# A hybrid mLSTM, differential attention and mixture-of-experts block: the router rebuilt around the output projection, and the odd experts' up matrix held whole

## The chip, the cores and the metric

The kernel runs on one core of a Trainium2 chip. The metric is the time of one execution on the device in microseconds (us), as the median of several runs. A core has TensorE (PE, matmuls; PEld is its loading of the stationary operand), VectorE (DVE), ScalarE (ACT), GpSimd (POOL), SyncE (SP, which here issues nearly all the transfers) and 16 DMA engines.

## What is computed

The block takes 256 rows of 1024, with 16 meta tokens ahead of them, and runs two branches and a mixture of experts. The part that the change touches is the end of the first half and the experts:

```python
h = layer_norm(DN_ALPHA * h + merged @ w_out[l], ln1_g[l], ln1_b[l])
# group_moe
probs = softmax(xt @ w_router)
sel = probs + router_bias
group_score = max(sel.reshape(-1, 4, 4), axis=-1); top_group = argmax(group_score)
_, idx = top_k(where(in_group, sel, NEG), 2)
w = probs at idx, divided by their sum
for e in range(16):
    h = silu(xt @ w_gate[e]) * (xt @ w_up[e])
    y = y + combine[:, e:e + 1] * (h @ w_down[e])
h = layer_norm(DN_ALPHA * h + ffn, ln2_g[l], ln2_b[l])
```

All inputs are float32. Each expert's three matrices are 1024 x 1024, 4 MiB each.

## The kernel before

**Projections.** Nine 1024 x 1024 sections (XM, OG, KA, QA, VA, GA, GB, WM, WA) and the output projection run one after the other. A weight piece of 128 x 512 is split on ScalarE and VectorE into a high part `whi` and a low part `wlo` (lines 667 and 968; 727 and 1037 for the output projection), and TensorE forms three products for each (lines 1562 to 1564; 1791 to 1793). There are four buffers for pieces. Attention and the mLSTM scan lie between and inside the sections.

**Output projection and LN.** The sixteen pieces of `w_out` go by rows: piece n is row block n // 2, column half n % 2, so all four accumulators (two row tiles of 128 tokens, two column halves) end together. After the last piece VectorE adds the residual into `h1` (L1334), takes the statistics (L1323), GpSimd raises to -0.5 (L627), VectorE normalises (L1341), and TensorE transposes (L1804). The transposed `h1t` gets the LN gain and bias on its way out of PSUM, half on VectorE (L1346), half on ScalarE (L887).

**Router.** Logits come as 16 x 256 (L1812), are copied and transposed back to 128 tokens x 16 (L1826). `h1t` is transposed back too (L1819) so that `h1` holds the finished rows. VectorE softmaxes and picks group and two experts by a chain of small operations (`first_max`, lines 1360 to 1368, three times) up to `mask` (L1421). Five small products turn the mask into each token's rank in its expert (L1834 to L1838), from which come `slot`, and `pick`, the 0/1 matrix that gathers up to 64 tokens for a unit. `keep_warm` issues matmuls on `ident` whose results nobody reads (L1537).

**Experts.** A unit is one block of 64 tokens of one expert; here there are 16, one for each expert. For each TensorE does the gate product (32 matmuls, L1895), the gather for the next unit (L1855), the up product (32), the scatter of the unit before (L1847), transposes (L1862), and the down product (32). `s.gate_used`, `s.up_used` and `s.down_used` count quarters of a product; SyncE waits on them before it reloads a buffer. SyncE works through one list in order. Buffers: `raw` has one slot each for gate, up and down; `gate_x` is a second gate buffer for the odd experts; `up_x` is a second buffer for the left half of up (its first 512 rows) of the odd experts. The right half of up has one buffer, so it is fetched only when the expert before has used it. The order of the list for expert e is gate (e + 1 or e + 2), up left, up right, down. Ahead of the router SyncE issues gate 0, up 0, gate 1 and down 0, then the two parts of `up_x`; the second of these waits for `h1_back`, and everything else for `units_ready`.

## Time and profile before

| | |
|---|---|
| median of 3 runs | 842.73 us (841.73 to 843.7) |
| the profiled execution, its own time | 843.29 us |
| its span in the profile | 841.0 us |
| TensorE busy | 785.0 us, 93% of the span |
| VectorE, ScalarE, GpSimd busy | 344.8, 242.5, 23.6 us |
| bytes read from HBM | 249.91 MB, 298 GB/s over the span |
| granted TensorE clock, mean | 0.99 |
| the chain that ended last | PE 67%, DMA 24%, DVE 4% |

The span runs from the first to the last recorded instruction; the execution's own time is 2.3 us longer. The chain is followed back from the last instruction, at each step to what released it. Line numbers are those of the kernel before. Times of day in a row ("382.19") are microseconds from the start of the span.

### The profile page before, as it was taken

The page shows a single profiled execution, that of the slowest core. Times are in us where ns is not written, and L with a number is a line of the kernel's source. Part 1 is how long each engine was busy: PE and PEld are TensorE (multiplying, and loading weights), DVE is VectorE, ACT ScalarE, POOL GpSimd, SP SyncE. Part 2 cuts the span into 40 slices and gives each one's busy share as a digit, 9 for nine tenths or more (in the row PEclk, how much of TensorE's full clock was granted, in tenths as well). Part 3 has the DMA queues.
Part 4 walks back from the last instruction along what each step waited for, and adds up shares of the span by engine and source line. Part 5 has one row for each costly group of instructions (what it writes and reads, how often), then busy time and mean ns, then how long its engine had stood idle before and what let it go on. Part 6 is the DMA issues. An engine that isn't in the chain of part 4 may idle for free.

```text
span 841.0 us, 12805 instructions
## 1 busy us (share of the span) xinstructions
PE 785.0 (93%) x4566; PEld 472.4 (56%) x4567; DVE 344.8 (41%) x765; ACT 242.5 (29%) x527; POOL 23.6 (3%) x49
## 2 busy tenths in 40 slices
PE   4999999999999999998999999998999989989983
PEld 3998679998889999873333332332333323323331
DVE  6676446554666778463222211220222202202225
ACT  2454423445666655231111011101110111011100
POOL 2002000000001000000000000000000000000000
PEclk9999999999999999999999999999999999999997
DMA  8965040555013544955999999999999999999991
GB/s 249 386 231 200 4 197 1 199 199 200 2 43 159 200 180 149 394 227 212 372 429 427 429 428 428 429 428 427 429 426 427 430 425 429 428 427 429 425 396 50
DMA packets 36219, 251.28 MB, mean 299 GB/s; under 512 B 5377, under 2 KB 12626, under 8 KB 22882
## 3 DMA queue, kind: packets, MB, share of 16 engines
q1 hardware_dynamic: 34128, 249.71, 72.5%
q10 hardware_dynamic: 2066, 1.25, 0.5%
q8 instruction: 14, 0.23, 0.1%
q14 instruction: 11, 0.09, 0.0%
HBM read 249.91 MB, written 1.05 MB: 298 GB/s over the span
## 4 chain that ended last, share of the span: by engine, by line
PE 67%; DMA 24%; DVE 4%; ACT 2%; issue 2%; POOL 1%; DVEq 0%; POOLq 0%; SPq 0%; ACTq 0%
DMA raw<-in_w_up_e_dram 24%; PE ps L1895 24%; PE ps L1562 8%; PE ps L1563 7%; PE ps L1564 7%; PE ps L1847 2%; PE ps L1855 2%; PE ps L1537 1%; PE ps L1618 1%; PE ps L1614 1%; PE ps L1674 1%; PE ps L1862 1%; PE ps L1791 1%; PE ps L1793 1%; PE ps L1792 1%
## 5 line engine op out<-in xcount | busy, mean ns | idle before, releaser
L1895 PE MATMUL ps<-raw,xg 128*64 128x512 f32 x640 | 146.2, 605 | 17.9 <-DMA raw<-in_w_up_e_dram 12.5
L1562 PE MATMUL ps<-hi_h,whi 128*128 128x256 f32 (+1 forms) x448 | 129.6, 289 | 2.6 <-DVE wlo L968 2.5
L1564 PE MATMUL ps<-hi_h,wlo 128*128 128x256 f32 (+1 forms) x448 | 127.4, 284 | 0.0
L1563 PE MATMUL ps<-lo_h,whi 128*128 128x256 f32 (+1 forms) x448 | 127.2, 284 | 0.0
L1895 PE MATMUL ps<-raw,hid 128*64 128x512 f32 x512 | 113.4, 595 | 0.0
L968 DVE TENSOR_TENSOR wlo<-raw,whi 128x512 fp32r<-128x512 f32 x144 | 93.5, 691 | 47.1 <-ACT whi L667 44.4
L1895 PEld LDWEIGHTS ps<-raw,xg 128*64 128x64 f32 x640 | 45.6, 139 | 115.2 <-issue 85.7
L1562 PEld LDWEIGHTS ps<-hi_h,whi 128*128 128x128 f32 x448 | 84.4, 188 | 7.2 <-DVE wlo L968 3.7
L667 ACT CAST whi<-raw 128x512 fp32r<-128x512 f32 (+1 forms) x144 | 83.3, 619 | 13.6 <-PE ps L1564 11.9
L1489 DVE TENSOR_TENSOR gs<-ps,gsig 128x512 f32<-128x512 f32 x16 | 11.1, 692 | 183.8 <-ACT gsig L915 183.8
L1564 PEld LDWEIGHTS ps<-hi_h,wlo 128*128 128x128 f32 x448 | 84.5, 189 | 0.0
L1563 PEld LDWEIGHTS ps<-lo_h,whi 128*128 128x128 f32 x448 | 84.3, 188 | 0.0
L1895 PEld LDWEIGHTS ps<-raw,hid 128*64 128x64 f32 x512 | 35.3, 137 | 67.3 <-issue 62.2
L1492 DVE TENSOR_TENSOR hs<-ps,gs 128x512 f32<-128x512 f32 x16 | 11.1, 692 | 134.6 <-PE ps L1895 134.6
L1895 PE MATMUL ps<-gate_x,xg 128*64 128x512 f32 x256 | 57.1, 595 | 5.3 <-DMA gate_x<-in_w_gate_e_dram 5.2
L919 ACT COPY hid<-ps 128x512 f32<-128x512 f32 x16 | 9.4, 586 | 160.3 <-PE ps L1862 160.3
L921 ACT COPY zsb<-ps 128x512 f32<-128x512 f32 x16 | 9.4, 586 | 115.0 <-PE ps L1895 115.0
L1895 PEld LDWEIGHTS ps<-gate_x,xg 128*64 128x64 f32 x256 | 17.9, 137 | 43.7 <-issue 33.1
L1498 DVE TENSOR_TENSOR acc<-ps,acc 128x512 f32<-128x512 f32 x64 | 39.8, 684 | 5.6 <-PE ps L1847 5.6
L915 ACT ACTIVATE gsig<-ps 128x512 f32<-128x512 f32 x16 | 9.6, 597 | 93.9 <-PE ps L1895 93.9
L1847 PE MATMUL ps<-zsb,wpt 64*128 64x512 f32 x136 | 33.8, 615 | 0.8 <-ACT zsb L921 0.8
L1855 PE MATMUL ps<-h,pick 128*64 128x512 f32 x136 | 32.1, 593 | 0.0
(311 smaller groups left out, 975.0 us busy)
## 6 DMA issues: line engine op xcount, KB each, us to landing
raw<-in_w_down_e_dram SPq DMA_DIRECT2D x32, 2048.0 KB, 21.7
raw<-in_w_up_e_dram SPq DMA_DIRECT2D x24, 2048.0 KB, 24.7
raw<-in_w_gate_e_dram SPq DMA_DIRECT2D x16, 2048.0 KB, 23.4
gate_x<-in_w_gate_e_dram SPq DMA_DIRECT2D x16, 2048.0 KB, 23.2
raw<-in_w_in_dram SPq DMA_DIRECT2D x28, 1024.0 KB, 9.2
up_x<-in_w_up_e_dram SPq DMA_DIRECT2D x16, 1024.0 KB, 27.5
raw<-in_w_branch_m_dram SPq DMA_DIRECT2D x4, 1024.0 KB, 8.1
raw<-in_w_branch_a_dram SPq DMA_DIRECT2D x4, 1024.0 KB, 8.0
```

Of the source, the lines that this page charges most:

```text
L667: act.copy(whi[:, b, :].rearrange("p (k c) -> p k c", c=P), piece(section, blk, kh)).then_inc(s.hi_ready, 1)
L915: act.activation(gsig[:], ps[:, B_GATE, :], ACT.Sigmoid).then_inc(s.gsig_ready, 1)
L968: dve.tensor_tensor(wlo[:, b, :].rearrange("p (k c) -> p k c", c=P), piece(section, blk, kh), whi[:, b, :].bitcast(F32).rearrange("p (k c) ...
L1489: dve.tensor_tensor(gs[:], ps[:, B_GATE, :], gsig[:], ALU.mult).then_inc(s.gs_ready, 1)
L1492: dve.tensor_tensor(hs[:], ps[:, B_UP, :], gs[:], ALU.mult).then_inc(s.hs_ready, 1)
L1498: dve.tensor_tensor(acc[:, t, cols], ps[:, B_SCAT[j], :], acc[:, t, cols], ALU.add).then_inc(s.acc_added, 1)
L1562: mm(o, w1, hi[:, k, c0:c0 + n], start=(k == 0), stop=False)
L1563: mm(o, w1, lo[:, k, c0:c0 + n], start=False, stop=False)
L1564: last = mm(o, w2, hi[:, k, c0:c0 + n], start=False, stop=(k == KB - 1))
L1847: mm(ps[:, B_SCAT[j], :], wpt[r0:r0 + SLOTS, t, :], zsb[r0:r0 + SLOTS, :], start=True, stop=True).then_inc(s.scat_done, 1)
L1855: last = mm(ps[r0:r0 + SLOTS, B_GATH, :], pick[:, t, 0:SLOTS], h1[:, t, 512 * c:512 * c + 512], start=(t == 0), stop=(t == TT - 1))
L1895: last = mm(ps[r0:r0 + SLOTS, bank_no, :], lhs[:, k % 4, k // 4, :], w[:, k % 2, 512 * c:512 * c + 512], start=(k == 0), stop=(k == KB - 1))
```

## The change

- **Output projection by column halves.** Pieces 0 to 7 are the left 512 columns, 8 to 15 the right. `residual_half` and `stats_half` of the left half are placed among VectorE's last splits, the transposes of the left half ahead of the last piece.
- **Logits from the un-normalised sum.** `h1` is transposed before it is normalised. The LN gain is multiplied into `wr`, its column mean is taken out, and the LN bias becomes a row `rout_b`; this is done among the KA, QA and VA sections. Logits come as 128 tokens x 16 and are scaled by rstd on VectorE.
- **All pairs compared.** In place of the three `first_max` chains every pair of a group, and every pair of groups, is subtracted and compared once, and the wins are summed.
- **Norm scale at the gather.** ScalarE normalises `h1` in place; the gain and bias are applied to the gathered and transposed `xg` (now two operations for each unit), and, spread over 128 partitions by 16 matmuls (`rows_b`), to `acc` in eight operations ahead of the loop. `h1` is no longer transposed back.
- **Up matrix whole.** `up_x_left` and two `up_x_right` buffers hold the whole up matrix of the odd experts. It is issued ahead of the router, and in the loop the order is gate, up, down. The two LN rows for the end move from ScalarE's list into SyncE's, behind the last expert.

The diff, cut to its core:

```diff
+    ht = at("ht", [P, KB, T], F + 8192)
...
-    up_x = (at("up_x0", [P, 2, D], split_area + 8192 - work),
-            at("up_x1", [P, 2, D], 0))
+    up_x_left = at("up_x_left", [P, 4, D], 0)
+    up_x_right = (at("up_x_right0", [P, 2, D], split_area + 8192 - work),
+                  at("up_x_right1", [P, 2, D], F + 23072))
...
-        for q, (read, n) in enumerate(((s.pieces_used, OUT_BASE + PIECES + NBUF), (s.h1_back, 2 * TT))):
-            sp.wait_ge(read, n)
-            sp.dma_start(flat(up_x[q][:]), flat(four_rows(w_up[0, 1], 0)[:, 2 * q:2 * q + 2, :])).then_inc(up_x_in[q], 16)
+        sp.dma_start(flat(up_x_right[1][:]), flat(four_rows(w_up[0, 1], 1)[:, 2:4, :])).then_inc(up_x_in[2], 16)
+        sp.wait_ge(s.pieces_used, OUT_BASE + PIECES + NBUF)
+        sp.dma_start(flat(up_x_left[:]), flat(four_rows(w_up[0, 1], 0))).then_inc(up_x_in[0], 16)
+        sp.dma_start(flat(up_x_right[0][:]), flat(four_rows(w_up[0, 1], 1)[:, 0:2, :])).then_inc(up_x_in[1], 16)
...
+        def fetch_up(e, odd):
+
+            last = last_block(e - 2)
+            sp.wait_ge(s.up_used, last * 4 + 2)
+            if odd:
+                sp.dma_start(flat(up_x_left[:]), flat(expert_rows(w_up, e, 0))).then_inc(up_x_in[0], 16)
+                for j in range(2):
+                    sp.wait_ge(s.up_used, last * 4 + (j + 3))
+                    sp.dma_start(flat(up_x_right[j][:]), flat(expert_rows(w_up, e, 1)[:, 2 * j:2 * j + 2, :])
+                                 ).then_inc(up_x_in[1 + j], 16)
+            else:
+                sp.dma_start(flat(raw_half(ESLOT[1], 0)), flat(expert_rows(w_up, e, 0))).then_inc(raw_in[ESLOT[1]][0], 16)
+                sp.wait_ge(s.up_used, last * 4 + 4)
+                sp.dma_start(flat(raw_half(ESLOT[1], 1)), flat(expert_rows(w_up, e, 1))).then_inc(raw_in[ESLOT[1]][1], 16)
+
+        def fetch_down(e):
+
             last = last_block(e - 1)
...
+        with sp.Fori(0, NE // 4 - 1) as i:
+            for odd in range(2):
+                fetch_gate(i * 2 + (2 + odd), odd)
+                fetch_up(i * 2 + (2 + odd), odd)
+                fetch_down(i * 2 + (1 + odd))
...
+        sp.wait_ge(s.gate_used, last_block(NE - 1) * 4 + 4)
+        for j, v in enumerate((ln2_g, ln2_b)):
+            sp.dma_start(rows1[:, j, :], v[0].partition_broadcast(P)).then_inc(s.rows2_in, 16)
...
-        for k in range(4, KB):
...
-        act.wait_ge(s.logit_done, 1)
-        act.copy(lgt[:], ps[0:NE, 4, 0:T]).then_inc(s.logit_sb, 1)
+        for b in range(4):
+            if b == 2:
+
+                act.activation(table_load[:], neglam[0:1, :], ACT.Exp)
+            act.wait_ge(s.ht_t1, b + 1)
+            act.copy(ht[:, 2 * b:2 * b + 2, :], turned1[:, 2 * b:2 * b + 2, :]).then_inc(s.ht_ready, 1)
+
...
-            for half in range(2):
-                act.wait_ge(s.h1_back, 2 * t + half + 1)
-                act.copy(h1[:, t, 512 * half:512 * half + 512], ps[:, 2 * t + half, :]).then_inc(s.h1_ready, 1)
-        for t in range(TT):
-            act.wait_ge(s.h1_ready, 2 * t + 2)
-            act.mul(acc[:, t, :], h1[:, t, :], ALPHA).then_inc(s.acc_ready, 1)
-
-        for j, v in enumerate((ln2_g, ln2_b)):
-            act.dma_start(rows1[:, j, :], v[0].partition_broadcast(P)).then_inc(s.rows2_in, 16)
+            act.activation(h1[:, t, :], h1[:, t, :], ACT.Identity, bias=nmr[:, t:t + 1],
+                           scale=rstd[:, t:t + 1]).then_inc(s.h1_ready, 1)
...
+        dve.wait_ge(s.wr_in, 16)
+        own(dve.tensor_tensor(wr_b[:], wr[:], l1b, ALU.mult))
+        own.settle()
+        own(dve.tensor_tensor(wr[:], wr[:], l1g, ALU.mult))
+        own(dve.tensor_reduce(rout_sum[:, 1, :], wr_b[:].rearrange("p k e -> p e k"), AX.X, ALU.add))
+        own.settle()
+        dve.tensor_reduce(rout_sum[:, 0, :], wr[:].rearrange("p k e -> p e k"), AX.X, ALU.add).then_inc(s.rout_in, 1)
...
+        dve.wait_ge(s.rout_done, 1)
+        dve.scalar_tensor_tensor(out=wr[:], in0=ps[:, 7, 0:NE].unsqueeze(1).to_broadcast([P, KB, NE]), scalar=-1.0 / D,
+                                 in1=wr[:], op0=ALU.mult, op1=ALU.add).then_inc(s.wr_ready, 1)
+        dve.tensor_copy(rout_b[:], ps[:, 7, NE:2 * NE]).then_inc(s.wr_ready, 1)
...
+        def residual_half(t, c):
+            dve.scalar_tensor_tensor(out=h1[:, t, 512 * c:512 * c + 512], in0=hres[:, t, 512 * c:512 * c + 512],
+                                     scalar=ALPHA, in1=ps[:, 4 + 2 * t + c, :], op0=ALU.mult,
+                                     op1=ALU.add).then_inc(s.resid_done, 1)
+
...
         for n in range(2, PIECES):
             split_out(n)
+            if n == KB + NBUF - 1:
+                dve.wait_ge(s.pieces_used, OUT_BASE + KB + NBUF)
+                residual_half(0, 0)
+            elif n == KB + NBUF:
+                residual_half(1, 0)
+            elif n in (KB + NBUF + 1, KB + NBUF + 2):
+                stats_half(n - (KB + NBUF + 1), 0)
+        dve.wait_ge(s.pieces_used, OUT_BASE + PIECES + NBUF)
+        for t in range(TT):
+            residual_half(t, 1)
+        for t in range(TT):
+            stats_half(t, 1)
+        own.settle()
+        for t in range(TT):
+            own(dve.bn_aggr(mv[:, t, :], stats[:, t, :, :]))
+        own.settle()
+        dve.tensor_scalar(ve[:, 0:TT], mv[:, 0:TT, 1], EPS, None, ALU.add).then_inc(s.var1, 1)
...
-        for t in range(TT):
...
-            dve.wait_ge(s.rstd1, t + 1)
-            dve.tensor_scalar(h1[:, t, :], h1[:, t, :], mv[:, t, 0:1], rstd[:, t:t + 1],
-                              ALU.subtract, ALU.mult).then_inc(s.xn1_ready, 1)
...
+        def take_gathered(n):
+            dve.tensor_tensor(xg[:], ps[:, B_XT, :].rearrange("p (a c s) -> p a c s", c=2, s=SLOTS), by_slot(gain4),
+                              ALU.mult).then_inc(s.xg_scaled, 1)
+            dve.wait_ge(s.xg_scaled, n)
+            dve.tensor_tensor(xg[:], xg[:], by_slot(bias4), ALU.add).then_inc(s.xg_ready, 1)
...
+        for t in range(TT):
+            own(dve.scalar_tensor_tensor(out=rt[:, 0, NE * t:NE * t + NE], in0=ps[:, t, 0:NE], scalar=rstd[:, t:t + 1],
+                                         in1=rout_b[:], op0=ALU.mult, op1=ALU.add))
         own.settle()
         dve.tensor_reduce(rt[:, 15, 0:TT], val(0), AX.X, ALU.max, negate=True).then_inc(s.router_exp, 1)
+        dve.wait_ge(s.rb_in, 16)
...
+        own(dve.tensor_reduce(best, sel8, AX.X, ALU.max))
+        own(dve.tensor_tensor(pair8, sel8.unsqueeze(2).to_broadcast([P, TG, EPG, EPG]),
+                              sel8.unsqueeze(3).to_broadcast([P, TG, EPG, EPG]), ALU.subtract))
+        own.settle()
...
+        dve.tensor_scalar(mask_b[:], val(12), 2.0, None, ALU.is_lt).then_inc(s.mask_ready, 1)
...
+        dve.wait_ge(s.rows_b, 1)
+        for t in range(TT):
+            for c in range(2):
+                cols = slice(512 * c, 512 * c + 512)
+                own(dve.scalar_tensor_tensor(out=acc[:, t, cols], in0=ps[:, 6 + c, :], scalar=ALPHA,
+                                             in1=h1[:, t, cols], op0=ALU.mult, op1=ALU.mult))
...
+        pe.wait_ge(s.rout_in, 1)
+        mm(ps[:, 7, 0:2 * NE], one[:].to_broadcast([P, P]), rout_sum[:].rearrange("p a e -> p (a e)"), start=True,
+           stop=True).then_inc(s.rout_done, 1)
...
+        def logits(half):
+
+            for k in range(4 * half, 4 * half + 4):
+                pe.wait_ge(s.ht_ready, max(k // 2 + 1, 2))
+                for t in range(TT):
+                    last = mm(ps[:, t, 0:NE], ht[:, k, P * t:P * t + P], wr[:, k, :], start=(k == 0), stop=(k == KB - 1))
+            return last
+
         for n in range(PIECES):
-            k, half = divmod(n, 2)
-            pe.wait_ge(s.mg_lo_s, k + 1)
+            half, k = divmod(n, KB)
...
+            if n == PIECES - 2:
+
+                pe.wait_ge(evac[WM], KB + 2)
+                pe.wait_ge(evac[WA], KB + 2)
+                turn_half(0)
+        logits(0)
+        turn_half(1)
+        logits(1).then_inc(s.logit_done, 1)
+
+
+        for r, b in ((C_L1G, (6, 7)), (C_L1B, (2, 4))):
+            for k in range(KB):
+                last = mm(ps[:, b[k // 4], P * (k % 4):P * (k % 4) + P], ident[0:81, r + k:r + k + 1].to_broadcast([81, P]),
+                          crow[:], start=True, stop=True)
+        last.then_inc(s.rows_b, 1)
+
+        keep_warm(5, 10)
 
         pe.wait_ge(s.mask_ready, 1)
         g = dict(skip_group_check=True)
-        mm(ps[:, 6, 0:NE], before[:], mask[:, 0, :], start=True, stop=True, **g)
...
+        ones_b = one_b[:].to_broadcast([P, P])
+        mm(ps[:, 5, 0:2 * NE], before_b[:], mask_b[:].rearrange("p t e -> p (t e)"), start=True, stop=False, **g)
+        mm(ps[:, 5, NE:2 * NE], ones_b, mask_b[:, 0, :], start=False, stop=True, **g)
+        mm(ps[:, 5, 2 * NE:3 * NE], ones_b, mask_b[:, 0, :], start=True, stop=False, **g)
+        mm(ps[:, 5, 2 * NE:3 * NE], ones_b, mask_b[:, 1, :], start=False, stop=True, **g).then_inc(s.rank_done, 1)
...
```

The VectorE program between the KA and the QA section (names: `stats`, `mv`, `ve` are the statistics of the mLSTM heads, `hh` their output). Before:

```order
L1190 BN_STATS stats_75<-hh 128x6
L1201 BN_AGGR mv_76<-stats_75 128x2 x8
L1203 TENSOR_SCALAR ve_77<-mv_76 128x8
L1011 UNCONDITIONAL_BRANCH
L1011 ISA
L968 ISA
L968 TENSOR_TENSOR wlo<-raw,whi 128x512
```

and now:

```order
L1205 BN_STATS stats_82<-hh 128x6
L1218 TENSOR_TENSOR wr_b<-wr,chan 128x128
L1220 TENSOR_TENSOR wr<-wr,chan 128x128
L1221 TENSOR_REDUCE rout_sum<-wr_b 128x16
L1223 TENSOR_REDUCE rout_sum<-wr 128x16
L1225 BN_AGGR mv_83<-stats_82 128x2 x8
L1227 TENSOR_SCALAR ve_84<-mv_83 128x8
```

Four operations have come in ahead of the aggregation, and so ahead of QA's next split.

The TensorE program from the last pieces of the output projection to the first gather (`h_135` and `h_142` are `h1`). Before:

```order
L1791 MATMUL ps<-whi,mg_hi 128x512
L1792 MATMUL ps<-whi,mg_lo 128x512
L1793 MATMUL ps<-wlo,mg_hi 128x512
L1537 MATMUL ps<-ident 128x128 x26
L1804 MATMUL ps<-ident,h_135 128x128 x16
L1812 MATMUL ps<-h1t,wr 16x256 x8
L1819 MATMUL ps<-ident,h1t 128x128 x8
L1826 MATMUL ps<-ident,lgt 128x16 x2
L1819 MATMUL ps<-ident,h1t 128x128 x8
L1537 MATMUL ps<-ident 128x128 x26
L1834 MATMUL ps<-mask,before 128x16
```

and now:

```order
L1870 MATMUL ps<-wlo,mg_hi 128x512
L1848 MATMUL ps<-ident,h_142 128x128 x8
L1868 MATMUL ps<-whi,mg_hi 128x512
...
L1870 MATMUL ps<-wlo,mg_hi 128x512
L1857 MATMUL ps<-wr,ht 128x16 x8
L1848 MATMUL ps<-ident,h_142 128x128 x8
L1857 MATMUL ps<-wr,ht 128x16 x8
L1884 MATMUL ps<-crow,ident 128x128 x16
L1592 MATMUL ps<-ident 128x128 x10
L1893 MATMUL ps<-mask_b,before_b 128x32
```

Half of the transposes now stand ahead of the last piece, those back are gone, and 16 products with `crow` and 10 on `ident` stand ahead of the rank products.

SyncE's list in the first lap of the loop, from gate to down. Before:

```order
L507 DMA gate_x<-in_w_gate_e_dram 128x4096
...
L526 DMA raw<-in_w_up_e_dram 128x4096
...
L530 DMA raw<-in_w_up_e_dram 128x4096
L532 REGISTER_ALU
L533 DMA raw<-in_w_down_e_dram 128x4096 x2
```

and now:

```order
L521 DMA gate_x<-in_w_gate_e_dram 128x4096
...
L532 DMA up_x_left<-in_w_up_e_dram 128x4096
L534 REGISTER_ALU
L535 DMA up_x_right_168<-in_w_up_e_dram 128x2048
...
L535 DMA up_x_right_169<-in_w_up_e_dram 128x2048
```

The odd expert's up matrix has moved into buffers of its own, so its right half no longer waits for the expert before; down follows it.

## Rows read from the trace of the kernel before

**Rows 1.** Windows: us; busy us of PE, PEld, DVE, ACT, POOL; PEclk, DMA share, GB/s.

```profile
378.00:386.00 8.00, 5.78 (x28) 2.09 (x26) 4.78 (x19) 1.87 (x2) 0.00 (x0) 1.00 0.00 2
382.20:408.00 25.80, 25.80 (x122) 9.49 (x124) 8.60 (x21) 1.77 (x3) 0.00 (x0) 1.00 0.72 268
386.00:389.00 3.00, 3.00 (x16) 1.04 (x14) 0.60 (x2) 0.00 (x0) 0.00 (x0) 1.00 0.72 208
408.00:816.00 408.00, 386.04 (x1788) 134.55 (x1786) 82.61 (x171) 54.00 (x74) 0.00 (x0) 0.99 1.01 428
818.00:819.00 1.00, 1.00 (x7) 0.39 (x8) 1.00 (x3) 0.00 (x0) 0.00 (x0) 1.00 0.27 115
```

**Rows 2.** Timeline, SyncE's queue: start, length, issue; x2 are two transfers.

```profile
349.62 0.80 SPq L487 DMA_DIRECT2D raw<-in_w_down_e_dram  x2
353.84 15.60 SPq L492 DMA_DIRECT2D up_x<-in_w_up_e_dram  x2
385.88 3.77 SPq L510 DMA_DIRECT2D raw<-in_w_gate_e_dram  x2
...
785.35 0.33 SPq L530 DMA_DIRECT2D raw<-in_w_up_e_dram  x1
```

**Rows 3.** The chain that ended last: start us, us, what.

```profile
442.61 6.87 PE ps L1895 x32
...
468.42 6.87 PE ps L1895 x32
...
811.12 3.65 PE ps L1895 x16
...
818.07 7.08 PE ps L1895 x32
```

**Rows 4.** Timeline of the router and first unit: start, us, engine, line, operation.

```profile
353.85 1.28 DVE L1334 SCALAR_TENSOR_TENSOR h<-hres,ps 128x512 f32<-128x512 f32 x2 [4.25 <-PE ps L1793]
...
362.04 1.09 PE L1804 MATMUL ps<-ident,h 128*128 128x128 f32 x8 [0.59 <-DVE h L1341]
...
368.33 0.19 DVE L1394 TENSOR_REDUCE rt<-rt 128x2 f32<-128x32 f32 x1
...
368.92 5.97 PE L1537 MATMUL ps<-ident 128*128 128x128 f32 x52
...
369.27 0.17 DVE L1397 RECIPROCAL rt<-rt 128x2 f32<-128x2 f32 x1 [0.76 <-ACT rt L895]
...
374.05 0.19 DVE L1421 TENSOR_TENSOR mask<-rt 128x32 f32<-128x32 f32 x1
...
374.73 0.29 PE L1834 MATMUL ps<-mask,before 128*128 128x16 f32 x2
...
375.95 0.19 DVE L1431 SCALAR_TENSOR_TENSOR slot<-ps,mask 128x32 f32<-128x32 f32 x1 [0.97 <-PE ps L1838]
...
377.28 1.94 PE L1855 MATMUL ps<-h,pick 128*64 128x512 f32 x8
...
380.69 0.69 DVE L1388 COPY xg<-ps 128x512 f32<-128x512 f32 x1 [1.46 <-PE ps L1862]
...
382.19 7.09 PE L1895 MATMUL ps<-raw,xg 128*64 128x512 f32 x32 [1.53 <-DVE xg L1388]
...
391.03 0.59 ACT L917 COPY xsb<-ps 128x512 f32<-128x512 f32 x1 [1.12 <-PE ps L1855]
```

**Rows 5.** Timeline: a small VectorE operation, and the start of QA.

```profile
22.97 0.29 DVE L1069 TENSOR_TENSOR lamp<-lamv 128x128 f32<-128x128 f32 x1
...
156.50 1.30 DVE L968 TENSOR_TENSOR wlo<-raw,whi 128x512 fp32r<-128x512 f32 x2 [2.11 <-POOL rstd L622]
...
157.25 0.39 PE L1562 MATMUL ps<-hi_h,whi 128*128 128x256 f32 x1 [0.49 <-DVE wlo L968]
```

**Rows 6.** Timeline of TensorE after a wait, and a window in it.

```profile
526.74 5.35 PE L1895 MATMUL ps<-raw,xg 128*64 128x512 f32 x16 [2.96 <-DMA raw<-in_w_up_e_dram]
...
528.00:529.00 1.00, 1.00 (x6) 0.31 (x4) 0.00 (x0) 0.00 (x0) 0.00 (x0) 0.50 1.08 459
```

287 lines of the change are left out of this document (126 added, 161 removed).

## The prediction

> **What bounds the kernel now.** I read the page's slices first, for where DMA is full, and then cut windows there. The program has two parts: up to 353.85 us TensorE streams projections, and from 408 us on the expert stage runs with saturated DMA, 428 GB/s over 408 to 816 us; the stream falls off in the window 818 to 819 [rows 1]. An expert has three matrices of 4 MiB. TensorE needs 25.81 us for a unit (442.61 to 468.42, from one up product to the next, where it waited for nothing) [rows 3], but 12 MiB at 428 GB/s take 29.4 us. The bytes are the bound, TensorE is not, and the end is
>
> (start of the first unit) + (bytes still to be moved) / rate + (time in which DMA moved nothing or little) + tail.
>
> I call the start of the first gate product s; before, s = 382.19 [rows 4]. The queue rows show what was loaded ahead of it: gate 0, gate 1, up 0, down 0 and the left half of up 1 in two parts (353.84 lasts to 369.4 because the second part waits for `h1_back`) [rows 2], 18 MiB. 174 MiB are left, 182.5 MB, 426.3 us at 428 GB/s. Lost after s: 3.8 us until 386 (the first gate buffer comes free at 385.88 [rows 2]), then 25.80 us ran at a mean of 268 GB/s from 382.2 to 408, which is 9.6 us of lost rate in all, the 3.8 included [rows 1]. The sum, 382.2 + 426.3 + 9.6 = 818.1, agrees with the fall-off in 818 to 819 [rows 1], so I trust this account. The tail: the last wait is for the right half of up 15, which was issued last but two (785.35 [rows 2]) and whose products start at 811.12; the last down product takes 818.07 to 825.15 [rows 3], and 15.85 us of output work follow to 841.0. By the byte account up 15's right half ends 4 MiB (9.8 us) before 818.3, at 808.5; TensorE went on 2.6 us later. I keep this 2.6 as the lag between a transfer's place in the byte account and its use.
>
> **The change, part by part.**
>
> *Router weights during the streams.* VectorE gets four operations on 128 x 128 elements between the last statistics of KA and the aggregation that QA waits for. One of that size is busy for 0.29, with the step to the next some 0.3 [rows 5]: 4 x 0.3 = 1.2 us. There VectorE is on the path: its wlo starts at 156.50 and TensorE waits for it until 157.25 [rows 5]. So +1.2. The small product with `rout_sum` adds one matmul between QA and VA, 0.23 (as a warm-up matmul, 5.97 / 26 [rows 4]). VectorE then waits for it, but has the length of a VA block as cover, so 0; without cover it would be 0.5. Together +1.45, and TensorE is busy from there to 353.85, so it all arrives. The added constants and small DMAs at the very start lie beside the wait for x and its statistics, with which TensorE starts: 0.
>
> *Output projection by halves.* The same 96 matmuls; the first half's residual and statistics move into VectorE's idle time, 0.64 each (1.28 for two [rows 4]) between the splits; the half is finished eight pieces ahead of the end, and a piece is six products of 512 columns, so there is room: 0, and 0.64 if the last split were late by one. Eight transposes go ahead of the last piece: 1.09 [rows 4] on TensorE, in the path.
>
> *Router.* Without the 1.45, from 353.85 [rows 4]: +1.09 = 354.94. Two residual halves (1.28) to 356.2; meanwhile the first 8 logit products, 0.23 each as the warm-up row, to 356.8. Eight transposes, 1.09, to 357.9; two copies of 128 x 512 on ScalarE, 0.59 each [rows 4], to 359.1; the last four logit products to 360.0. Variance and rstd run beside this on VectorE and GpSimd and are done by about 359. After the logits there are two races. VectorE: two scale-and-add and one maximum (0.65), exponentials and return 0.94 (as before between maximum 368.33 and reciprocal 369.27 [rows 4]), then up to the mask 8 small operations at 0.217 (369.27 to 374.05 were 22 of them [rows 4]) and three of 128 elements at 0.3, 2.7 us: mask at 364.3, where it took 4.8 before. TensorE: 16 matmuls that spread the gains plus 10 warm-up ones, 26 in all as before, 5.97 [rows 4]: until 366.0. TensorE is later, so 1.7 of what VectorE saves is lost; if a matmul with a broadcast stationary row costs half, the mask decides at 364.3. I take 366.0, since the form is nearest to the warm-up row. Four rank products instead of five: 1.22 (374.73 to the slot operation at 375.95) becomes 0.8 (bounds 0.6, half for the narrower type, and 1.0, four fifths): 366.8. Slot to gather was 1.33 (375.95 to 377.28) and loses one small operation: 367.9. Gather to first product was 4.91 (377.28 to 382.19 [rows 4]). The second operation of `take_gathered`, 0.69, lies in the 0.8 between xg's end at 381.38 and 382.19, in which TensorE was still reading its registers: 0, at most 0.7. So 372.8, and with the 1.45, **s = 374.3, 7.9 us earlier.**
>
> *Up matrix whole.* Before s there are now 20 MiB: at 351 us down 0 and one quarter of up 1, from 356.4 the other three. 8 MiB take 19.6 us and are through at about 373, ahead of s + 3.7. In place of 174, 172 MiB remain after s: 180.4 MB, 421.4 us. In each lap the order is gate, up, down. By the rows of the first unit the buffers come free at s + 3.7, 7.4 (gate), 12.3, 15.7 (up), 22.6, 26.4 (down), and 2 MiB take 4.9 us; starting at s + 5.35 the transfers end at 10.3, 15.2, 20.1, 25.0, 29.9, 34.8, each after the next is issued. So what the stretch to 408 lost besides vanishes (between 389 and 408, while up 1's right half and down 1 were issued into an empty queue), and only the first loss stays: 3.8 plus 3 us at 208 GB/s, 1.55 [rows 1]: 5.35. Last byte: 374.3 + 5.35 + 421.4 = 801.05.
>
> *Tail.* Up 15 now comes ahead of down 15, but down 15 is issued only when down 14 is used. TensorE's last wait is thus for down 14, which has 8 MiB behind it: 801.05 - 19.6 + 2.6 = 784.05. Then half a down product (3.5), a whole unit (25.8) and 15.85 of output: 829.2. Up 15 (793.9) and down 15 (803.7) arrive before they are wanted (796 and 806). The tail after the last byte grows from 22.9 to 28.15 us, and takes back part of the gain. The two LN rows (1 MiB) move behind down 15, 2.5 us, needed 20 us later: 0. The eight operations that form `acc` (8 x 0.69) end at s + 11, the scatter needs them at s + 15.7: 0.
>
> *Sum.* -7.9 (s) -4.9 (2 MiB) -4.25 (lost rate: 9.6 - 5.35) +5.25 (tail) = -11.8; 829.2 against 841.0. The profiled execution took 843.29 with a span of 841.0, the median of the runs is 842.73, 1.73 over the span. I predict 842.7 - 11.8, **831.0 us**.
>
> Beside this stands a page. "DMA: Bandwidth & Descriptors" of the Trainium skill (Anatomy of one DMA) gives each transfer a fixed cost of about 2.0 us, mostly between the last byte and the semaphore. Put in for my 2.6, which this trace shows, it would make 830.4, by that page's figure.
>
> **Rivals.**
>
> 1. *The queue still runs dry in the first laps.* For it: my transfers end only about a microsecond after the next issue in the first unit (down 1 at s + 26.4 against 29.9, gate 3 at s + 29.7 against 34.8, and up 1's half at 23.8 to 25.0 against 22.6). Against: with each lap 3.6 us of backlog are added. One of the two dips (4.25 / 2 = 2.1 us) or both: 833 to 835.5.
>
> 2. *The half clock.* After a wait of 3 us TensorE ran sixteen products in 5.35 us instead of 3.65 (526.74 against 811.12) [rows 3, 6], with a granted clock of 0.50 at 528 to 529 [rows 6], the 1.2 GHz level. Now each unit waits 3.6 us for down, and after down 14 there is no slack: +1.7. Of 58 matmuls that only kept TensorE busy around the router 48 are gone; if the first gate product ran at half clock, its first buffer would come free up to 3.5 us later. 832.5 to 836. "TensorE: Matmul & The Clock Gate" (What's actually happening) of the Trainium skill says that the throttled state is the default and activity lifts it; the row at 526.74 agrees. Against it: the wait splits in two (2.2 for the first half of down, 1.4 for the second), and the longest gap that I find in the new router is 1 us.
>
> 3. *Slower.* SyncE serves its list strictly in order, and down now stands behind the whole up matrix of the next expert. If a unit's down is issued with nothing in the queue, every expert pays a restart of about 2.1 us: 14 x 2.1 = 29 us against the 11.8, 848. It decides from the sixth restart on. Against it: at that point the queue holds gate and up of the next expert, 8 MiB or 19.6 us by my schedule.
>
> 4. *No change.* The stage is bound by bytes, so a faster router would be worth nothing if DMA's restart did not hang on it. But 378 to 386 shows 2 GB/s [rows 1], and 385.88 is the first gate buffer's release: the restart does hang on s.
>
> **How the numbers follow.** The forecast 0.77, rival 1 0.10, rival 2 0.07, rival 3 0.04, rival 4 0.02. The forecast's own spread: 1.7 less if the mask decides the rank, 2.6 less if the lag at down 14 is nothing, 0.7, 0.64 and 0.5 more for the covers that I priced at nothing: 827 to 833. With rivals 1 and 2: 825.5 to 836. A difference of 0.2% (1.7 us) is about what this kernel's runs can tell. Faster by more 0.94, within 0.02, slower 0.04.
>
> **What would show it.** First gate product at 374 to 375; TensorE late by 1.4 at the start of the output projection; DMA idle only until s + 3.8, with no window under 400 GB/s from s + 7 on; last byte near 801; down 14's second half as the last DMA in the chain, and 45 us from there to the end. Wrong if s is late because the added VectorE work costs more than 1.45, if DMA windows in the first laps dip, or if the last units wait for anything but down.

## The result, and the profile after

The median went from 842.73 to **838.21 us** (five runs, 835.42 to 838.64), a ratio of 0.9934 with an interval of 0.9913 to 0.9955. The forecast was 831.0 us with a range to 836.0: the direction was right, the gain is 4.5 us where 11.7 were forecast, and the time lies outside the range. The profiled execution took 835.89 us with a span of 834.1.

The expert stage first, since the account of [rows 1] rests on it. These are windows of the kernel after; the columns are as there:

```profile
374.00:382.90 8.90, 6.49 (x30) 2.43 (x32) 6.61 (x27) 1.87 (x2) 0.00 (x0) 1.00 0.01 4
383.00:386.00 3.00, 3.00 (x16) 1.04 (x14) 2.20 (x5) 0.00 (x0) 0.00 (x0) 1.00 0.70 191
...
389.00:408.00 19.00, 18.95 (x92) 7.16 (x90) 7.19 (x14) 2.46 (x3) 0.00 (x0) 1.00 1.00 428
408.00:806.00 398.00, 378.72 (x1762) 135.95 (x1760) 91.50 (x183) 52.13 (x72) 0.00 (x0) 0.99 1.01 428
806.00:809.00 3.00, 3.00 (x16) 1.06 (x14) 0.77 (x2) 0.00 (x0) 0.00 (x0) 1.00 0.83 336
```

DMA is idle until SyncE gets the first gate buffer at 382.94, needs three microseconds to come up, and then moves 428 GB/s from 389 to 806 with no dip in the first laps. The last weight bytes land near 806, the norm's two rows behind them. In this stage TensorE waits for one matrix only, down; the second line is its wait ahead of the first gate product. The waits are given by cause (us in total, times, longest), then the chain that ended last:

```profile
PE ps L1952 <- DMA raw<-in_w_down_e_dram: 18.9, 12, 2.1
...
PE ps L1952 <- DVE xg L1413: 1.7, 1, 1.7
```

```profile
757.92 25.63 DMA raw<-in_w_down_e_dram
783.55 0.04 issue
783.59 15.65 PE ps L1952 x64
...
811.18 7.11 PE ps L1952 x32
```

The chain enters TensorE's last unbroken stretch by down 14's transfer at 783.59, and not by an up half as before [rows 3]. That matrix was forecast, but this is its first half, 50.5 us from the end; the forecast had the second half, and 45 us. The timeline there and a window in it, and below them the same two products in experiment 9:

```profile
783.59 8.78 PE L1952 MATMUL ps<-raw,hid 128*64 128x512 f32 x32 [2.08 <-DMA raw<-in_w_down_e_dram]
```

```profile
784.00:788.00 4.00, 4.00 (x14) 1.20 (x12) 0.60 (x2) 0.00 (x0) 0.00 (x0) 0.57 1.01 430
```

```profile
775.87 3.65 PE L1961 MATMUL ps<-raw,hid 128*64 128x512 f32 x16 [1.84 <-DMA raw<-in_w_down_e_dram]
780.76 3.65 PE L1961 MATMUL ps<-raw,hid 128*64 128x512 f32 x16 [1.23 <-DMA raw<-in_w_down_e_dram]
```

In the kernel after the granted clock is down behind this wait, as rival 2 had it, and the two halves take 8.78 us without a wait between them. In experiment 9 the clock stays up and TensorE waits 1.23 us for the second half instead. From the start of the first half to the end of the span it is 50.5 us and 50.3: the half clock there takes 0.2 us and not 1.7, since it runs in time that would be a wait.

Now the router: the timeline of the kernel after, to be held against [rows 4]. A float32 matmul leaves two records here, so x32 is 16 of them and x20 is 10; a transpose or a bf16 matmul leaves one.

```profile
357.00 1.85 PE L1857 MATMUL ps<-wr,ht 128*128 128x16 f32 x16
358.70 1.07 PE L1848 MATMUL ps<-ident,h 128*128 128x128 f32 x8
360.22 2.94 PE L1857 MATMUL ps<-wr,ht 128*128 128x16 f32 x16 [0.46 <-ACT ht L912]
363.00 7.17 PE L1884 MATMUL ps<-crow,ident 81*128 81x128 f32 x32
369.96 3.00 PE L1592 MATMUL ps<-ident 128*128 128x128 f32 x20
372.80 0.18 PE L1893 MATMUL ps<-mask_b,before_b 128*128 128x32 bf16 x1
...
374.04 1.94 PE L1913 MATMUL ps<-h,pick 128*64 128x512 f32 x8 [0.99 <-DVE pick L1397]
...
379.09 5.37 PE L1952 MATMUL ps<-raw,xg 128*64 128x512 f32 x24 [1.68 <-DVE xg L1413]
```

```profile
366.96 0.18 DVE L1463 TENSOR_SCALAR mask_b<-rt 128x32 bf16<-128x32 f32 x1
...
373.09 0.19 DVE L1470 SCALAR_TENSOR_TENSOR slot<-ps,mask 128x32 f32<-128x32 f32 x1 [5.54 <-PE ps L1896]
```

```profile
360.00:362.00 2.00, 1.78 (x12) 1.78 (x12) 0.33 (x2) 0.66 (x2) 1.42 (x3) 0.75 0.94 401
362.00:370.00 8.00, 8.00 (x39) 8.00 (x39) 3.21 (x18) 2.95 (x6) 0.00 (x0) 0.50 1.02 431
370.00:372.00 2.00, 2.00 (x14) 2.00 (x14) 0.00 (x0) 0.00 (x0) 0.00 (x0) 0.69 0.94 397
```

The windows are read for their third column from the end, the granted clock: 0.75 over two microseconds is one microsecond at half clock, so the clock fell at about 361.0, stayed at 0.50 (the 1.2 GHz level) and came back at about 371.2 (0.69 over the last two). TensorE was busy in nearly all of that time. The 16 row matmuls took 7.17 us and the 10 warm-up ones 3.00, from 363.0 to 372.8 together 9.8, where I had put 5.97. VectorE had the mask at 367.14 and then waited 5.54 us. The first gate product, s in the prediction, starts at 379.09 and not at 374.3.

### The profile page after: what moved, and what is told of

Same layout as the page of the kernel before. It is cut to its first block, busy times and chain, and to the rows that moved or that the text cites. A ratio compares the mean times of both kernels' runs of the same rounds, so it can differ in the third digit from the quotient of the medians.

```text
span 834.1 us, 12681 instructions
## 1 busy us (share of the span) xinstructions
PE 779.0 (93%) x4496; PEld 474.1 (57%) x4497; DVE 357.6 (43%) x780; ACT 240.8 (29%) x523; POOL 22.7 (3%) x51
## 4 chain that ended last, share of the span: by engine, by line
PE 71%; DMA 21%; DVE 3%; ACT 2%; issue 2%; POOL 1%; DVEq 0%; POOLq 0%; SPq 0%; ACTq 0%
PE ps L1952 26%; DMA raw<-in_w_down_e_dram 21%; PE ps L1617 8%; PE ps L1619 7%; PE ps L1618 7%; PE ps L1905 2%; PE ps L1913 2%; PE ps L1673 1%; PE ps L1920 1%; PE ps L1669 1%; PE ps L1729 1%; PE ps L1592 1%; PE ps L1868 1%; PE ps L1870 1%; PE ps L1869 1%
## 5 line engine op out<-in xcount | busy, mean ns | idle before, releaser
L1952 PE MATMUL ps<-raw,hid 128*64 128x512 f32 x512 | 119.6, 618 | 19.4 <-DMA raw<-in_w_down_e_dram 18.9
L1952 PE MATMUL ps<-raw,xg 128*64 128x512 f32 x512 | 112.7, 592 | 1.7 <-DVE xg L1413 1.7
L1952 PEld LDWEIGHTS ps<-raw,xg 128*64 128x64 f32 x512 | 37.3, 137 | 73.8 <-issue 73.8
```

The costliest lines, as they stand in the source:

```text
L1952: last = mm(ps[r0:r0 + SLOTS, bank_no, :], lhs[:, k % 4, k // 4, :], w[:, k % 2, 512 * c:512 * c + 512], start=(k == 0), stop=(k == KB - 1))
```

## The experiments

The times of one kernel scatter here by several microseconds between its own runs, and the profiled start of the kernel by 1.9. So beside each median stand three figures of the profile: s, the start of the first gate product; the span; and their difference, which the scatter ahead of s does not touch. "Half clock in the router" is worked out from windows of 1 us, as above. Each kernel's median stands with its lowest and highest run; the kernel before, run beside them, had medians of 843.0 to 843.4. The expectations were reckoned from 838.21 for the kernel after; all nine of its runs (the five above and the four of experiment 11) have the median 835.89, 2.3 us less.

| kernel | median, runs | ratio to before (interval) | half clock in the router | s | span | span - s |
|---|---|---|---|---|---|---|
| before | 842.73 | | none | 382.19 | 841.0 | 458.8 |
| after | 838.21 (835.42 to 838.64) | 0.9934 (0.9913 to 0.9955) | 10.2 | 379.09 | 834.1 | 455.0 |
| 1 warm-up first | 832.84 (831.26 to 835.87) | 0.9874 (0.9857 to 0.9891) | 3.4 | 374.51 | 831.3 | 456.8 * |
| 2 no warm-up | 835.80 (832.66 to 837.00) | 0.9896 (0.9880 to 0.9912) | 13.7 | 377.74 | 834.3 | 456.6 * |
| 3 warm-up in the middle | 833.21 (831.41 to 839.22) | 0.9885 (0.9860 to 0.9911) | none | 374.50 | 831.3 | 456.8 * |
| 4 fetch order of before | 837.65 (835.83 to 842.30) | 0.9939 (0.9918 to 0.9959) | 10.2 | 379.38 | 837.6 | 458.2 |
| 5 gaps filled with rows | 830.53 (827.80 to 831.56) | 0.9842 (0.9826 to 0.9858) | 6.8 | 374.29 | 829.1 | 454.8 |
| 6 plain operand | 838.59 (832.96 to 838.73) | 0.9944 (0.9929 to 0.9959) | 6.8 | 376.20 | 831.4 | 455.2 |
| 7 gaps filled, warm-up | 832.16 (830.86 to 833.94) | 0.9874 (0.9857 to 0.9890) | 3.4 | 374.26 | 829.2 | 454.9 |
| 8 VectorE work moved | 835.39 (833.44 to 836.28) | 0.9909 (0.9894 to 0.9924) | 10.2 | 376.72 | 831.7 | 455.0 |
| 9 best | 827.92 (827.51 to 828.47) | 0.9823 (0.9809 to 0.9836) | none | 371.43 | 826.2 | 454.8 |
| 10 full rows | 832.60 (831.29 to 835.84) | 0.9884 (0.9865 to 0.9902) | none | 373.33 | 830.0 | 456.7 * |
| 11 after again | 835.69 (833.48 to 838.58) | 0.9905 (0.9890 to 0.9920) | 13.7 | 379.98 | 836.8 | 456.8 * |
| 12 before, less warm-up | 847.55 (846.03 to 848.16) | 1.0057 (1.0043 to 1.0070) | 6.8 | 383.44 | 843.8 | 460.4 * |

The star marks profiles in which the clock was down in the first gate product as well.

My theory: the changed router lets TensorE's clock fall, and its 16 row matmuls do not bring it back. Rivals: a fall has its own length whatever is issued; the fetch order gave less than forecast; the start of the kernel became slower.

**1. The warm-up first.**

```diff
+        keep_warm(5, 10)
         for r, b in ((C_L1G, (6, 7)), (C_L1B, (2, 4))):
...
-        keep_warm(5, 10)
```

> The kernel after with one move: the 10 warm-up matmuls stand ahead of the 16 matmuls that repeat the norm's rows, not behind them; the same 26 matmuls in all. In the kernel after these 26 took 9.8 us (363.0 to 372.8) with the granted clock at 0.50 until about 370.7, and the rank product behind them was 5.7 us later than VectorE's mask. Theory A (the clock comes back when the warm-up's plain 128x128 matmuls run, and the 16 broadcast matmuls do not bring it back): back at full clock about 0.7 us into the warm-up, near 364; the 26 take about 6.5 us, rank product near 369.5, time 3.0 to 3.4 us under the kernel after: 835.0. Theory B (once fallen, the clock stays down for some 10 us whatever is issued): full clock again near 370.7 as before, rank product at 372.8, time 838.2.

Timeline of TensorE, and a window with its granted clock:

```profile
360.71 3.80 PE L1592 MATMUL ps<-ident 128*128 128x128 f32 x20
364.30 4.09 PE L1886 MATMUL ps<-crow,ident 81*128 81x128 f32 x32
368.22 0.18 PE L1893 MATMUL ps<-mask_b,before_b 128*128 128x32 bf16 x1
...
374.51 8.78 PE L1952 MATMUL ps<-raw,xg 128*64 128x512 f32 x32 [1.68 <-DVE xg L1413]
```

```profile
375.00:379.00 4.00, 4.00 (x14) 1.30 (x12) 2.33 (x7) 0.00 (x0) 0.00 (x0) 0.57 0.01 4
```

The same 26 matmuls take 7.5 us, and the 16 row matmuls run at full speed once the clock is back. A fall has no fixed length, so theory B falls. Four of the five runs lie under the fastest of the nine runs of the kernel after (833.48), the fifth does not. New is a second fall, in the first gate product: 8.78 us instead of 7.09 [rows 4], and span - s is 1.8 larger.

**2. No warm-up:** the line `keep_warm(5, 10)` is taken out.

> The kernel after without its 10 warm-up matmuls in the router (no result comes from them). The 16 row matmuls end at 370.2 at half clock; VectorE's mask is there at 367.1, so the rank product starts at 370.2 instead of 372.8. Theory A (it was the warm-up that brought the clock back): half clock goes on through the rank product, the gather and the turn into the first gate product, which gives back 0.7 to 1.5 us: 836.3 to 837. Theory B (the clock comes back at about 370.7 by itself): the 2.6 us are gained whole: 835.6.

```profile
361.00:374.00 13.00, 12.01 (x53) 9.60 (x53) 6.27 (x38) 2.95 (x6) 0.45 (x2) 0.50 0.94 398
```

The clock does not come back by itself at 371; it stays down through the rank product and the gather, and falls again in the first gate product. By the windows this is theory A. The time alone does not tell: 835.80 is nearer to B's 835.6 than to A's 836.3 to 837, and it equals the 835.89 of the nine runs of the kernel after, so the 2.6 us that the matmuls took are not gained. Nor is the length of the fall by itself the mark of the missing warm-up, since experiment 11 has 13.7 us with the warm-up in place.

**3. Warm-up in the middle.**

```diff
         logits(0)
+        keep_warm(3, 8)
         turn_half(1)
```

> The kernel after with 8 more warm-up matmuls (0.23 us each at full clock, 1.84 us) between the first and the second half of the logits, where the clock was still full. Theory A (the stretch of transposes and 16-column products lets the clock fall): with the 8 in its middle the clock stays at 1.00 through the router, the 26 matmuls take 5.97 instead of 9.8 us, so 1.84 paid and 3.8 gained: 836.2, and the granted clock 1.00 from 357 to 380. Rival (the fall has another cause, as the DMA's 430 GB/s beside it): the clock falls anyway and the time is 840.0.

```profile
357.00:375.00 18.00, 14.19 (x115) 11.92 (x116) 10.11 (x49) 5.90 (x10) 1.42 (x3) 1.00 0.84 355
```

At full clock the 26 matmuls took 362.32 to 368.21, 5.9 us: the 5.97 of my prediction, with DMA as busy as in the kernel after, so it isn't DMA that holds the clock down. One of the six runs took 839.22. It has no profile, but its mean granted clock, 0.978 over a span of 837.5 against 0.987 over 831.3, makes some 15 us more of half clock (2 x 0.022 x 837.5 = 37 against 22). Where these lay is not recorded; if in the router, the eight matmuls don't always suffice. And experiment 10 below shows no fall in the router without them, so one profile does not prove that they hold the clock.

**4. The fetch order of before**, with the changed router: an odd expert's second up half waits for the previous expert's up product again, and expert 1's is not prefetched.

```diff
-                fetch_gate(i * 2 + (2 + odd), odd)
-                fetch_up(i * 2 + (2 + odd), odd)
-                fetch_down(i * 2 + (1 + odd))
...
+            fetch_gate(i * 2 + 3, True)
+            fetch_rest(i * 2 + 2, False)
+            fetch_gate(i * 2 + 4, False)
+            fetch_rest(i * 2 + 3, True)
```

> The kernel after with the fetch order of the kernel before: an odd expert's up matrix arrives in its own buffers still, but the second half is issued only behind the previous expert's up product, in two transfers, expert 1's second half is not prefetched, and the gate is asked for ahead of it as in the kernel before. The router is the changed one. My sum gives the whole up matrix 4.9 (2 MiB already there) + 4.25 (no loss at the laps' start) - 5.25 (longer tail) = 3.9 us, so 842.1. Rival (the fetch order is worth nothing, all of the gain is the router's): 838.2. Rival (the order costs as much as the router gave): above 844.

TensorE's waits in the expert stage, in us, times, longest:

```profile
PE ps L1956 <- DMA up_x_right<-in_w_up_e_dram: 8.6, 5, 3.0
PE ps L1956 <- DMA raw<-in_w_up_e_dram: 5.0, 4, 1.8
PE ps L1956 <- DMA gate_x<-in_w_gate_e_dram: 4.7, 5, 1.2
```

The waits for up and gate are back and that for down is gone. Span - s is 458.2 against 455.0: the new order is worth **3.2 us**, where my terms made 4.9 + 4.25 - 5.25 = 3.9. The medians do not show it as well: 837.65 is far from my 842.1, nearer to the first rival's 838.2, and 1.8 above the 835.89 of the nine runs, with runs from 835.83 to 842.30. By span - s neither rival holds; by the time alone the first would not be excluded.

**5 and 7. TensorE's gaps filled.** 7 puts plain warm-up matmuls into the three gaps behind the rank product; 5 puts the row matmuls there, and only 12 matmuls stay ahead of the rank product.

```diff
         keep_warm(5, 10)
+        norm_rows(0, 2)
...
+        norm_rows(2, 6)
...
         pe.wait_ge(s.pick_ready, TT)
...
         gather()
+        norm_rows(6, 9)
...
         turn_rows(B_XT, xsb[:], s.xt_done)
+        norm_rows(9, 2 * KB)
```

(7: `keep_warm(1, 4)`, `(1, 3)` and `(1, 7)` in these places, all 16 rows behind the first warm-up.)

> The kernel after with its 10 warm-up matmuls ahead, and the 16 row matmuls (whose result is needed only when the accumulator is built) spread: 2 behind the warm-up, 4 behind the rank product, 3 behind the gather, 7 behind the turn of the gathered rows, so in TensorE's gaps of 0.99, 0.69 and 1.68 us. In the run with the warm-up first the rank product was ready to start 4.0 us after the logits' end (VectorE's mask, near 364.8) but TensorE came to it at 368.2, and the clock fell again for 3.3 us at 375.6 in the first gate product (about 1.7 us lost). Theory A (work with gaps and narrow products lets the clock fall, each fall costs what is done in it at half speed): rank product near 365.5, no fall near 375, first gate product 3 us earlier than 374.5 and at full clock, time 4 to 5 us under 832.8: 828. Rival (the fillers delay the chain as much as they give, and the fall comes anyway): 831 to 833.

> The kernel with the warm-up first (832.8) plus plain warm-up matmuls in TensorE's gaps of the router's end: 4 behind the rank product (0.92 us in a gap of 0.99), 3 behind the gather (0.69 in 0.69), 7 behind the turn (1.6 in 1.68). Nothing on the path should be later by more than 0.2 us. Theory A: the fall of 3.3 us at 375.6 in the first gate product, which cost about 1.7 us, goes: 831.2, granted clock 1.00 from 365 to 390. Rival (that fall has nothing to do with the gaps): 832.8, the fall stays.

Windows of 7, then of 5:

```profile
365.00:388.00 23.00, 22.88 (x137) 12.17 (x137) 13.95 (x42) 3.05 (x4) 0.00 (x0) 1.00 0.70 282
```

```profile
361.00:367.00 6.00, 6.00 (x29) 6.00 (x30) 2.84 (x17) 2.96 (x6) 0.57 (x2) 0.50 1.01 429
368.00:388.00 20.00, 19.81 (x109) 9.14 (x109) 13.95 (x42) 3.05 (x4) 0.00 (x0) 1.00 0.72 291
```

With the gaps filled there is no second fall in either, and the first gate product takes 7.09 again; beside experiment 1 span - s is 1.9 us less. That the filling did it is not shown: of the ten profiles with these gaps as they were, six have the second fall and four (after, 4, 6, 8) have not, and the three with filled gaps (5, 7, 9) have none. By medians 7 gains 0.7 on experiment 1, half of what I expected, and 5, with 830.53, missed the 828 of theory A and lies just under its rival's 831. In 5 the first fall lasted 6.8 us in this profile although the warm-up began at 362.9, so the rank product came at 367.93 and not at 365.5; one of its runs had 827.80.

**6 and 10. What the 16 matmuls are.** 6 uses a plain piece of the identity, `ident[0:81, :]`, in place of the repeated column; 10 makes each of the 16 a product of the 128 x 128 identity with itself. Both leave out the norm's rows, so what follows works on other values.

> The kernel after with a plain 81x128 piece of the identity as the stationary operand of the 16 row matmuls, in place of one column of it repeated 128 times: same count, same moving operand, same shape of the product, other values (the rows of the norm's gain and bias, and with them the accumulator, are then wrong; all timing stays). Theory A1 (it is the repeated column that doesn't bring the clock back): full clock again some 3.5 us after the fall at 361, near 364.5, the 16 and the 10 behind them end near 369.8, rank product 3 us earlier than 372.8, time 835.2 against 838.2. Theory A2 (it is not the operand; the clock comes back only at the warm-up's 128-row matmuls or 10 us after the fall): half clock until 370.7 as before, time 838.2.

> The kernel after with each of its 16 row matmuls replaced by a plain product of the 128x128 identity with itself into the same place (the norm's rows, and with them the accumulator, are left out), so 26 full 128-row matmuls stand behind the logits. Theory A2 (matmuls of 81 rows do not bring the clock back, those of 128 do): half clock from 361 ends near 364.5 to 367, the 26 end at 368 to 370 instead of 372.8, time 833 to 835.5, and no run at 838. Rival (the kind of matmul does not matter, only when the fall begins): times of both kinds as before, 835.5 and 838.4, and the row matmuls' stretch at half clock for 7 us again.

```profile
360.76 6.16 PE L1884 MATMUL ps<-crow,ident 81*128 81x128 f32 x32
366.72 3.35 PE L1592 MATMUL ps<-ident 128*128 128x128 f32 x20
```

```profile
357.00:373.00 16.00, 12.52 (x101) 10.53 (x100) 9.96 (x48) 6.13 (x12) 1.42 (x3) 1.00 0.98 415
373.00:377.00 4.00, 3.67 (x10) 1.18 (x12) 3.15 (x10) 0.05 (x1) 0.00 (x0) 0.57 0.06 20
```

In 6 (rows above first) the clock came back at 368.7, 2.0 us into the warm-up and not at 364.5: with the plain piece, too, the clock stayed down as long as the row matmuls ran, so the repeated column is not the reason, and A1 falls. Its six runs are two of 833.0 and four of 838.6. In 10 no run lies above 835.84, and in its profile the clock did not fall until 373.0, just ahead of the first gate product, though its program is that of the kernel after until 361.15. That agrees with A2, that matmuls of 81 rows do less for the clock; but A2 expected a fall at 361 that ends early, and there was none. Since whether a fall comes differs from run to run, and the values differ too, experiments 6 and 10 do not prove that it is the 81 rows.

**8. The VectorE work moved.** The router's four operations between KA and QA stand behind the signal for the heads' rstd, in VectorE's wait for GpSimd.

```diff
-        own(dve.tensor_tensor(wr_b[:], wr[:], l1b, ALU.mult))
...
         dve.tensor_scalar(ve8[:], mv8[:, :, 1], EPS, None, ALU.add).then_inc(s.var8, 1)
+        own(dve.tensor_tensor(wr_b[:], wr[:], l1b, ALU.mult))
...
         dve.wait_ge(s.rstd8_ready, 1)
```

> The kernel after with the router's four VectorE operations between the KA and the QA section moved behind the signal for GpSimd's rstd of the heads, into the wait for it (2.1 us). My term of +1.2 us for this insertion: the QA section's evacuations come 1.2 us earlier by the trace (162.4 to 161.2 against the KA ones), so does all behind them, time 1.2 under the kernel after: 837.0 (in the trace the piece 7 signal 356.0 where the start of the kernel is the same). Rival (the insertion hides behind TensorE, and the 1.2 us is lost elsewhere): 838.2 and no shift.

VectorE in the kernel after, and then in this one:

```profile
154.19 0.29 DVE L1218 TENSOR_TENSOR wr_b<-wr,chan 128x128 f32<-128x128 f32 x1
...
158.38 1.29 DVE L983 TENSOR_TENSOR wlo<-raw,whi 128x512 fp32r<-128x512 f32 x2 [2.11 <-POOL rstd L642]
```

```profile
153.06 0.65 DVE L1216 BATCH_NORM_AGGREGATE mv<-stats 128x2 f32<-128x6 f32 x8
...
156.02 1.29 DVE L983 TENSOR_TENSOR wlo<-raw,whi 128x512 fp32r<-128x512 f32 x2 [0.88 <-POOL rstd L642]
```

From the first operation behind KA's statistics (there the first of the four, at 154.19, here the aggregation, at 153.06) to the next wlo it is 4.19 us there and 2.96 here, 1.23 less; VectorE's wait shrinks by as much, from 2.11 to 0.88. From the first product to the output projection's end it is 333.0 and 331.8. That is my term of 1.2, and it is on the path. The medians, 835.39 against 835.89, are too scattered to show it.

**9. Best:** experiment 5, with 8's edit, and `keep_warm(6, 4)` between `turn_half(1)` and `logits(1)`.

> The version that puts together what the runs showed: warm-up ahead and the 16 row matmuls in TensorE's gaps (830.5), the four VectorE operations behind the signal for the heads' rstd (1.25 us earlier by the trace), and 4 more warm-up matmuls (0.92 us) between the second turn and the second half of the logits, of which 0.46 lies in a wait. Theory A: if these 4 keep the clock up through the logits, the second half of them takes 1.96 instead of 2.96 us and the warm-up ends before the mask: first gate product at 371.5 to 372, time 827.5. Rival (the clock falls anyway, only later): the VectorE move alone counts, less the 0.46: 829.7.

```profile
360.88 2.48 PE L1592 MATMUL ps<-ident 128*128 128x128 f32 x20
...
365.07 0.19 PE L1899 MATMUL ps<-mask_b,before_b 128*128 128x32 bf16 x1 [1.27 <-DVE mask_b L1463]
```

```profile
357.00:388.00 31.00, 29.56 (x182) 16.79 (x183) 19.76 (x68) 7.09 (x12) 1.42 (x3) 1.00 0.87 362
```

827.92 us where 827.5 was expected, 1.8% under the kernel before, and the five runs lie within 1.0 us where those of the kernel after span 3.2, and all nine of them 5.2. The rank product now waits for VectorE's mask, so TensorE is no longer late. The clock is full from 357 to 388. Which of the two additions did how much was not separated: if 1.2 of the 2.6 under experiment 5 is 8's, the rest is the 4 matmuls' or the runs' own difference.

**11. After again.**

> The kernel after, unchanged, to see what differs between its own executions. If the start of the kernel is noise (x's landing and the moment when the clock first rises), the first evacuation will stand anywhere within 1.8 us of the 27.5 seen, without a change of code; end minus first gate product should be 455.0 where that product runs at full clock and 456.8 at half. Time: 835.5 or 838.4, median 837.

```profile
362.73 7.17 PE L1884 MATMUL ps<-crow,ident 81*128 81x128 f32 x32
369.70 4.16 PE L1592 MATMUL ps<-ident 128*128 128x128 f32 x20
...
379.98 8.36 PE L1952 MATMUL ps<-raw,xg 128*64 128x512 f32 x30 [1.68 <-DVE xg L1413]
```

This profile is of an 838.58 run: 13.7 us of half clock in the router instead of 10.2, and a second fall in the first gate product. Against the first profile that is 0.9 us more at s and 1.8 in span - s, together the 2.7 between the two times. So these two runs differ by how long the clock is down.

**12. The kernel before with the warm-up of after.**

```diff
-        keep_warm(0, 26)
...
-        keep_warm(7, 26)
+        keep_warm(7, 10)
...
-        keep_warm(7, 6)
```

> The kernel before with its warm-up cut to that of the kernel after: the 26 matmuls behind the output projection and the 6 ahead of the gather taken out, the 26 ahead of the rank product cut to 10. No result comes from them, and TensorE waited for VectorE behind all three. Theory A (it was the 58 warm-up matmuls that held the clock at 1.00 through the router of before, and the change took 48 of them away): the granted clock falls to 0.50 within 357 to 382, and the time is 1 to 4 us more: 844.5 to 847. Rival (the clock's fall is due to the changed router's narrow logit products): clock 1.00, time 843.3.

```profile
360.21 3.32 PE L1803 MATMUL ps<-ident,h 128*128 128x128 f32 x16 [6.64 <-DVE h L1341]
...
377.05 3.45 PE L1854 MATMUL ps<-h,pick 128*64 128x512 f32 x8 [1.21 <-DVE pick L1378]
```

```profile
356.00:363.00 7.00, 2.79 (x13) 2.77 (x14) 5.54 (x12) 0.00 (x0) 2.32 (x4) 0.52 0.98 417
...
376.00:381.00 5.00, 3.45 (x8) 0.77 (x8) 2.78 (x19) 0.46 (x1) 0.00 (x0) 0.66 0.23 94
```

The time is 4.6 us more (847.55 against 843.0, expected 844.5 to 847) without 48 matmuls that have no result. The clock falls in the old router too: in the wait of 6.64 us, behind the mask, and in the first gate product. So a fall does not need the narrow logit products of the new router. But here the first two falls come in or behind waits of 6.64 and 2.96 us, and in the new router TensorE had no wait over 0.46 us there; why the clock falls in that place stays open.

## Why the prediction was wrong

**The step that failed** is the TensorE side of the race ahead of the rank product: "16 matmuls that spread the gains plus 10 warm-up ones, 26 in all as before, 5.97: until 366.0". I read a duration from a stretch at full clock, in a router with 58 warm-up matmuls, and carried it over to a router from which the change takes 48 of them. The 26 ran at half clock until 371.2 and took 9.8 us, +3.8; in experiment 3, at full clock, they took 5.9. The second half of the logits, in which the clock fell, took 2.94 instead of 1.96 (experiment 1), about +1.0. The output projection ended 0.8 later than forecast (0.6 of it the start's scatter), and other steps were 0.8 shorter (0.5 of it behind the rank product): together the 4.8 by which s came late. Behind s the sum came as forecast: the prediction's 829.2 + 4.8 is 834.0, the span is 834.1. There the last wait was for the first half of down 14 and not the second, and 0.2 us went to a half clock that the forecast left out, so the agreement to a tenth is luck.

**Rival 2 named the mechanism, in the wrong places, and my argument against it was wrong.** It put the half clock in the first gate product and behind down 14, not in the matmuls ahead of the rank product, and its 832.5 to 836 does not hold 838.21 either. I said that the longest gap in the new router is 1 us, as if only gaps could lower the clock. The windows show TensorE busy for 1.78 of the 2.00 us in which it fell, and for 8.00 of 8.00 at 0.50. Of its prices, "up to 3.5 us" in the first gate product holds as a bound: it costs 1.8 in the profiles in which it happens. The profile of experiment 11 has it, in a run of 838.58, so it may be part of why the median (838.21) is above the profiled run (835.89); the four runs behind that median have no profile. The 1.7 behind down 14 came out as 0.2. The span missed by 4.9, and the median lies 2.3 above the profiled run: together the miss of 7.2.

"TensorE: Matmul & The Clock Gate" of the Trainium skill (What's actually happening) has the throttled state as the default, which activity releases. Experiment 12 agrees, where a wait of 6.64 us ends with the clock at 0.50. Its picture of long waits as the cause (HAM oscillation), taken alone, would have left the changed router at full clock; by this case's windows an engine that the profile calls busy can lose the clock, and the measurement decides. The same page of the Trainium skill (Part 4) says that transposes in TensorE's transpose mode do not count as busy in the same way. The changed router has eight of them ahead of the second half of the logits; no run here isolates them.

**Point by point.** *Start: 0.* Holds. The 0.6 us by which the profile of after starts later is scatter: the first products start at 24.19 in it, at 22.88 in experiment 1, whose program is the same up to there, and at 23.54 before. *Weights during the streams: +1.45, and 8 transposes +1.09.* From the first product to the output projection's end: 330.3 before, 333.0 after, +2.7 for 2.54; experiment 8 shows the VectorE part singly. *Output projection by halves: 0.* Holds. *Mask:* 3.98 us behind the logits' end, forecast 4.3. *Rank to first gate product:* 6.3, forecast 6.8. *Fetch:* the 3.9 measured 3.2 (experiment 4). *Rate and last byte:* s + 426.75 gives 805.8, the windows 806. *Last wait:* down 14, but its first half. *Rival 1:* cut into windows of 5 us from 386 on, none is under 406 GB/s; single microseconds go down to 344. *Rival 3:* it did not happen, DMA moved 428 GB/s from 408 to 806; its 848 is also a wrong sum, for 831.0 and 29 make 860. *Rival 4:* the restart of DMA moved with s. *The 2.0 us of the Trainium skill* ("DMA: Bandwidth & Descriptors", Anatomy of one DMA) instead of 2.6: too small a difference to see here; besides, that section gives the figure for transfers issued by GpSimd, and these are SyncE's.

With full clock in the router the working was good to about 1 us: experiments 3 and 10 have s at 374.5 and 373.3 for the 374.3 forecast. Their first products came 0.8 and 0.3 us earlier than in the kernel before, and experiment 3 has 1.84 us of matmuls more; with both reckoned out, s is near 373.5. Both then lose 1.8 us in the first gate product.
